# One core, two transformer blocks and a 32-expert layer in fp32: the router's chain, the first gather, the residual and one weight unit rearranged

## What is computed

```python
h = h + mixed @ w_out                       # (256,1024) @ (1024,1024)
xt = rms_norm(h, norm2_gain)
group_logits = xt @ w_route_group + b_g     # 4 groups
exp_logits = xt @ w_route_expert + b_e      # 32 experts, 8 a group
g_idx = argmax(group_logits)                # one group a token
top_v, top_i = top_k(exp_logits[g_idx], 2)  # two experts in it
w = softmax(top_v) * softmax(group_logits)[g_idx]
for e in experts:                           # D_EXPERT = 512
    y[tokens of e] += w * ((silu(xt @ w_gate[e]) * (xt @ w_up[e])) @ w_down[e])
return rms_norm(h + y, final_gain)
```

## Time and profile before

| | |
|---|---|
| median of 3 runs | 1062.4 us (1061.07 to 1064.08) |
| the profiled execution's own time | 1058.74 us |
| its span | 1056.7 us |
| busy: PE, DVE, ACT, POOL | 86%, 42%, 30%, 2% of the span |
| HBM read | 290.77 MB, mean 279 GB/s with what is written |
| chain that ended last, by engine | PE 54%, DMA 35%, DVE 6%, ACT 2% |

### The profile page before, as it was taken

The page is one execution under the profiler, slowest core; times in us unless marked ns, Lnnn a source line. Parts: engine busy times, 40 slices in busy tenths (PEclk is TensorE's granted clock), DMA queues, the critical chain, the costliest instruction groups (busy, mean ns, idle before and its releaser), DMA issues.

```text
span 1056.7 us, 18049 instructions
## 1 busy us (share of the span) xinstructions
PE 908.8 (86%) x7830; PEld 647.1 (61%) x7830; DVE 441.0 (42%) x555; ACT 317.3 (30%) x400; POOL 19.0 (2%) x36
## 2 busy tenths in 40 slices
PE   5999999999999999999989997676868577677875
PEld 5999988999998878999978732121313122121311
DVE  4677778666565448995757400000101000010102
ACT  4466664643443337544522300000000000000001
POOL 1300000000000000000000100000000000000000
PEclk9999999999999999999998998999889989898888
DMA  9993424456545354442057899999999999999994
GB/s 338 269 351 110 160 81 160 159 182 204 173 163 220 136 199 160 160 161 80 5 201 263 356 370 421 421 421 422 421 422 421 422 421 421 421 422 421 423 421 183
DMA packets 83398, 294.97 MB, mean 279 GB/s; under 512 B 5887, under 2 KB 33167, under 8 KB 58624
## 3 DMA queue, kind: packets, MB, share of 16 engines
q1 hardware_dynamic: 78240, 284.18, 68.9%
q10 hardware_dynamic: 3552, 6.08, 1.6%
q0 software_dynamic: 1536, 3.68, 1.3%
HBM read 290.77 MB, written 4.10 MB: 279 GB/s over the span
## 4 chain that ended last, share of the span: by engine, by line
PE 54%; DMA 35%; DVE 6%; ACT 2%; SPq 2%; issue 1%; DVEq 0%; ACTq 0%
DMA arena<-in_w_down 16%; PE psum L960 13%; PE psum L962 13%; PE psum L961 13%; DMA arena<-in_w_gate 10%; DMA arena<-in_w_up 8%; PE psum L1485 3%; PE psum L1280 3%; SPq L813 2%; PE psum L1505 2%; PE psum L935 1%; DVE ring_rounded L1942 1%; PE psum L927 1%; PE psum L1035 1%; PE psum L1474 1%
## 5 line engine op out<-in xcount | busy, mean ns | idle before, releaser
L1485 PE MATMUL psum<-arena,featL 128*32 128x512 f32 x1024 | 181.6, 692 | 63.4 <-DMA arena<-in_w_up 47.1
L1942 DVE TENSOR_TENSOR ring_rounded<-arena,hi_rounded 128x2048 fp32r<-128x2048 f32 x77 | 176.0, 2290 | 91.2 <-ACT hi_rounded L1590 90.1
L1590 ACT ACTIVATE hi_rounded<-arena 128x2048 fp32r<-128x2048 f32 x77 | 146.6, 1912 | 156.6 <-PE psum L962 52.1
L960 PE MATMUL psum<-hi_rounded,featT_rounded 128*128 128x256 f32 (+1 forms) x560 | 165.5, 296 | 5.9 <-DVE featL_rounded L1958 3.9
L961 PE MATMUL psum<-ring_rounded,featT_rounded 128*128 128x256 f32 (+1 forms) x560 | 163.2, 291 | 0.0
L962 PE MATMUL psum<-hi_rounded,featL_rounded 128*128 128x256 f32 (+1 forms) x560 | 163.1, 291 | 0.0
L1485 PEld LDWEIGHTS psum<-arena,featL 128*32 128x32 f32 x1024 | 40.8, 122 | 197.5 <-DMA arena<-in_w_up 87.1
L1505 PE MATMUL psum<-arena,featT 128*32 128x512 f32 x496 | 89.1, 653 | 41.1 <-DMA arena<-in_w_down 36.3
L960 PEld LDWEIGHTS psum<-hi_rounded,featT_rounded 128*128 128x128 f32 x560 | 108.6, 194 | 9.3 <-DVE ring_rounded L1942 4.2
L961 PEld LDWEIGHTS psum<-ring_rounded,featT_rounded 128*128 128x128 f32 x560 | 108.8, 194 | 1.2
L962 PEld LDWEIGHTS psum<-hi_rounded,featL_rounded 128*128 128x128 f32 x560 | 108.6, 194 | 1.3
(11 more groups left out here) (282 smaller groups left out, 1138.4 us busy)
## 6 DMA issues: line engine op xcount, KB each, us to landing
arena<-in_w_gate SPq DMA_DIRECT2D x75, 1024.0 KB, 26.2
arena<-in_w_up SPq DMA_DIRECT2D x75, 1024.0 KB, 26.6
arena<-in_w_down SPq DMA_DIRECT2D x63, 1024.0 KB, 26.9
arena<-in_w_in SPq DMA_DIRECT2D x14, 2048.0 KB, 9.1
arena<-in_w_down SPq DMA_DIRECT2D x5, 2048.0 KB, 7.6
arena<-in_w_out SPq DMA_DIRECT2D x4, 2048.0 KB, 8.3
arena<-in_w_in SPq DMA_DIRECT2D x4, 1024.0 KB, 9.7
t_copies<-arena ACTq DMA_DIRECT2D x1, 2048.0 KB, 8.2
```

The lines of the kernel that those rows point to most:

```text
L960: mm(o, lhs[0], rhs[0], start=start, stop=False, skip_group_check=True)
L1485: ins = mm(psum[32 * j:32 * j + 32, MB[4 + m], :], xg[:, 4 * half + k, 32 * j:32 * j + 32], quad[place(q)][j][:, 512 * k:512 * k + 512], s ...
L1590: fn(high, view, ACT.Copy).then_inc(hi_ready, 1)
L1942: tt(low, view, high.bitcast(F32), ALU.subtract).then_inc(lo_ready, 1)
```

## The change

Five things are changed.

1. The second unit of `wo2` is stored as two blocks of 256 columns, each by a DMA of its own. A block is then free as soon as its own chunk is done, so quad 3's piece 0 is issued behind `wo2` (1, 0). Quad 3's piece 3, which goes where the rounded chunk (0, 1) was, is issued behind `wo2` (0, 1).
2. PE starts `ybank` with identity times `x`, in place of the products of zeros; the zeroing on POOL and the four fillers ahead of them are gone. The final add on DVE is gone, and ACT and DVE read `ybank` in PSUM.
3. Since `x` is then free, quad 5's piece 0 goes there, and no longer waits for `pieces_read` but for those products (`scattered`) and for `xn`.
4. The router: ACT squares 768 columns ahead and 256 at the end; PE adds the logits of the first 256 columns ahead of the last transposes; both tiles' ranks are in one bank, come before the count, and DVE turns them into `rank` and `G` before it touches the count; fillers go from six to three.
5. The gather has three steps (slices 0-1, 2-3, 4-7); the third stands behind the first 16 gate products.

At the end ACT squares halves of 512 columns from PSUM and adds their sums through the bias of the root.

```diff
+    add("dve", "rank")
     add("dve", "count")
-    for t in range(NT):
-        add("dve", "rank", t)
...
+        quad.append([x[:].rearrange("p t d -> p (t d)")])
...
-        for n in range(2):
-            unit(("wo2", n), (0, DK, 512, kxn(A["w_out_2"], 512 * n, 512)))
+        unit(("wo2", 0), (0, DK, 512, kxn(A["w_out_2"], 0, 512)))
+        unit(("wo2", 1), (0, DK, 256, kxn(A["w_out_2"], 512, 256)), (2048, DK, 256, kxn(A["w_out_2"], 768, 256)))
...
+        ONCE = (2, 1, 1, 1)
+
+        def once(r, pair, q, j):
+            return isinstance(r, int) and isinstance(pair, int) and pair * 12 + q < NQ + ONCE[j]
+
+        def quad_place(r, pair, q, j):
 
             if not isinstance(r, int):
                 return PLACES[q % NQ]
-            if isinstance(pair, int) and pair * 12 + q <= NQ:
-                return (*PLACES, NQ)[q]
-            return PLACES[(q - 1) % NQ]
...
+            if once(r, pair, q, j):
+                return (*PLACES, NQ, NQ + 1)[q]
+            return PLACES[(q - ONCE[j]) % NQ]
...
+        GATHERS = ((6, (0, 1)), (5, (2, 3)), (7, (4, 5, 6, 7)))
+        GATHERED_AT = ((0, 0), (0, 2), (1, 0))
...
                     wait_filled(sp, "wo2", 0, 1)
                     load_quad(0, 0, 2, pieces=range(3))
+                    load_quad(0, 0, 3, pieces=(3,))
                     wait_filled(sp, "wo2", 1, 0)
                     load_quad(0, 0, 2, pieces=(3,))
+                    load_quad(0, 0, 3, pieces=(0,))
                     wait_filled(sp, "wo2", 1, 1)
-                    load_quad(0, 0, 3)
+                    load_quad(0, 0, 3, pieces=(1, 2))
                     wait_filled(sp, "logit", NT - 1)
                     load_quad(0, 0, NQ, pieces=(3,))
-                    for q in range(NQ + 1, 12):
-                        load_quad(0, 0, q, 4 * (q - NQ - (q <= 2 * NQ)))
+                    sp.wait_ge(xn_ready, 2 * NT)
+                    sp.wait_ge(scattered, 2 * NT)
+                    load_quad(0, 0, NQ + 1, pieces=(0,))
+                    load_quad(0, 0, NQ + 1, pieces=(1, 2, 3))
+                    for q in range(NQ + 2, 12):
+                        load_quad(0, 0, q, 4 * (q - NQ))
...
+            add_logits(0)
+            wait_emptied(pe, "wo2", 1, 1)
+            for k in range(2):
+                for t in range(NT):
+                    ins = tr(last_T[:, NT * k + t, :], x[:, t, (6 + k) * P:(7 + k) * P], ident)
+            end(ins)
+            for j in range(1, 4):
+                add_logits(j)
...
-            busy(4)
-            pe.wait_ge(gt_ready, 1)
             for t in range(NT):
                 for n in range(2):
-                    ins = mm(ybank[t, n], GT[:, t, :], dd[:, n, :], start=True, stop=False, skip_group_check=True)
+                    ins = mm(ybank[t, n], ident, x[:, t, 512 * n:512 * n + 512], start=True, stop=False, skip_group_check=True)
                     ins.then_inc(scattered, 1)
 
+            b = begin("rank")
+            pe.wait_ge(route_ready, 1)
+            mm_halves(b[:, 0:E], con("before"), selr[:, 0, :], True, True)
+            mm_halves(b[:, E:2 * E], con("ones"), selr[:, 0, :], True, False)
+            end(mm_halves(b[:, E:2 * E], con("before"), selr[:, 1, :], False, True))
...
-            busy(6)
-            wait_emptied(pe, "rank", NT - 1)
+
+
+            busy(3)
+            wait_emptied(pe, "rank")
...
+                pe.wait_ge(onehot_ready, n + 1)
+                gather(0)
+                gather(1)
                 for m in range(2):
                     for half in range(2):
-                        pe.wait_ge(xg_ready, 2 * n + half + 1)
+                        if m == 0 and half == 1:
+                            if isinstance(n, int) and n == 0:
+                                wait_emptied(pe, "count")
+                            gather(2)
                         q = 6 * gp + 2 * m + half
                         for k in range(4):
+                            if m == 0 and (half, k) in GATHERED_AT:
+                                pe.wait_ge(xg_ready, 3 * n + GATHERED_AT.index((half, k)) + 1)
...
+            wait_emptied(act, "wo2", 1, 0)
+            for t in range(NT):
+                part = st[:, 14 + t:15 + t]
+                a.link(fn(xn[:, t, 0:768], x[:, t, 0:768], ACT.Square, accum_out=part))
+                a.link(fn(part, part, ACT.Identity, scale=1.0 / D, bias=eps_col[:, 0:1]))
+            wait_emptied(act, "wo2", 1, 1)
+            for t in range(NT):
+                s = st[:, 6 + t:7 + t]
+                a.link(fn(xn[:, t, 768:], x[:, t, 768:], ACT.Square, accum_out=s))
+                fn(s, s, ACT.Sqrt, scale=1.0 / D, bias=st[:, 14 + t:15 + t]).then_inc(rms_ready, 1)
...
-            for n in range(2):
-                for t in range(NT):
-                    dve.wait_ge(scattered, 4 * NG + (2 * n + t + 1))
-                    xs = x[:, t, 512 * n:512 * n + 512]
-                    tt(xs, xs, psum[:, MB[2 * t + n], :], ALU.add).then_inc(resid_done[t], 1)
```

More of the change, by code:

```diff
@@ L334, in build @@
     who_of = dict(fills)
-    last = {index[key] % 8 for key in (("rank", 0), ("rank", 1), ("count",))}
+    last = [index[key] % 8 for key in (("rank",), ("count",))]
     MB = [b for b in range(8) if b not in last]
-    MB += sorted(last)
+    MB += last
     with ExitStack() as ctx:
@@ L673, in build @@
             chunk(("p2", n // 2), n % 2, cols256(("p2", n // 2), n % 2), ring[(n + len(RW_ORDER)) % 3], ("p2", n // 2, n % 2))
-        for n in range(4):
-            chunk(("wo2", n // 2), n % 2, cols256(("wo2", n // 2), n % 2), W_RING[n % 3], ("wo2", n // 2, n % 2))
+        for c in range(2):
+            chunk(("wo2", 0), c, cols256(("wo2", 0), c), W_RING[c], ("wo2", 0, c))
+        for c in range(2):
+            chunk(("wo2", 1), c, lambda of, c=c: wview(("wo2", 1), c, of), W_RING[(2 + c) % 3], ("wo2", 1, c))
         before, taken = [], {}
@@ L1416, in _, with add_logits @@
                     resid_T(3, j - 1, ("wo2", (j - 1) // 2, (j - 1) % 2))
-            resid_T(3, 3, ("wo2", 1, 1))
+            last_T = begin("nt", 3, 3).rearrange("p (k q) -> p k q", q=P)
             logits = [begin("logit", t) for t in range(NT)]
-            for j in range(4):
+            def add_logits(j):
                 wait_emptied(pe, "nt", 3, j)
@@ L1485, in moe_group @@
                                 ins = mm(psum[32 * j:32 * j + 32, MB[4 + m], :], xg[:, 4 * half + k, 32 * j:32 * j + 32],
-                                         quad[place(q)][j][:, 512 * k:512 * k + 512], start=half == 0 and k == 0,
+                                         quad[place(q, j)][j][:, 512 * k:512 * k + 512], start=half == 0 and k == 0,
                                          stop=half == 1 and k == 3, skip_group_check=True)
@@ L1505, in down @@
                     return mm(psum[32 * j:32 * j + 32, MB[4 + half], :], hhT[:, k, 32 * j:32 * j + 32],
-                              quad[place(q)][j][:, at_:at_ + 512], start=k == 0, stop=k == 3, skip_group_check=True)
+                              quad[place(q, j)][j][:, at_:at_ + 512], start=k == 0, stop=k == 3, skip_group_check=True)
                 q = 6 * gp + 4
@@ L1879, in _ @@
                         moe_round(r)
-            squares(4, lambda t: act.wait_ge(resid_done[t], 2))
+                        act.wait_ge(scattered, r * (4 * NG) + (4 + 4 * NG))
+                        fn(st[:, 12:13], eps_col[:, 0:1], ACT.Copy)
+            fn(warm[:], eps_col[:, 0:1], ACT.Sqrt)
+            for n in range(2):
+                for t in range(NT):
+                    act.wait_ge(scattered, 4 * NG + (2 * n + t + 1))
+                    s, half = st[:, 8 + t:9 + t], st[:, 10 + t:11 + t]
+                    a.link(fn(xn[:, t, 512 * n:512 * n + 512], psum[:, MB[2 * t + n], :], ACT.Square,
+                              accum_out=s if n else half))
+                    if n == 0:
+                        fn(half, half, ACT.Identity, scale=1.0 / D, bias=eps_col[:, 0:1]).then_inc(squared, 1)
+                    else:
+                        act.wait_ge(squared, t + 1)
+                        fn(s, s, ACT.Sqrt, scale=1.0 / D, bias=half).then_inc(rms_ready, 1)
         @block.vector
@@ L2405, in _, with one_hot @@
             red(e2, m2g, AX, ALU.add).then_inc(e2_ready, 1)
+            wait_filled(dve, "rank")
+            dve.wait_ge(route_ready, 1)
+            empty(stt(rank, bank("rank")[:, 0:NT * E].rearrange("p (t e) -> p t e", t=NT), CHOSEN, selr, ALU.add, ALU.mult), "rank")
+            def one_hot(es):
+                slots = con("slot").unsqueeze(1).unsqueeze(1).to_broadcast([P, NT, EG, CAP])
+                tt(G, slots, rank[:, :, es].unsqueeze(3).to_broadcast([P, NT, EG, CAP]), ALU.is_equal).then_inc(onehot_ready, 1)
+            one_hot(slice(0, EG))
             wait_filled(dve, "count")
             empty(red(rt[:, 606:607], bank("count")[:, 0:E], AX, ALU.max), "count")
+            nc.vector.tensor_copy(cnt[:, 0:1], rt[:, 606:607]).then_inc(count_ready, 1)
```

(12 more changed lines are left out.)

69 lines of the change are left out of this document (33 added, 36 removed).

## The result

The changed kernel took 1053.78 us (median of 4 runs, 1053.47 to 1054.92) beside 1062.52 us for the kernel before (4 runs, 1061.07 to 1064.08): the medians are 8.7 us apart, and the recorded ratio is 0.9925, 95% interval 0.9903 to 0.9946, which is 8.0 us less. In a later series on one chip it was 1053.85 us (6 runs) beside 1061.73 us (21 runs), 7.9 us less, ratio 0.9923 (0.9900 to 0.9946). The forecast was 6.7 us less, at 1055.7 us, with a range from 1052.8 to 1058.9.

What follows compares the result with a forecast made beforehand. The experts' part was taken to be bound by the stream of weights. Stream -6.5, stragglers +0.6 and norm -0.8 gave -6.7 us, so 1062.4 - 6.7 = 1055.7 us, with a range from 1052.8 to 1058.9.

Steps and rivals of the forecast that it cites:

- the two holes: Stretches 589 to 593 and 606 to 612, where the weight stream stands still; together 7.04 us, the most it can give.
- Hole A: 589 to 593, ended when quad 3 can go out; 2.25 us lost, closed by issuing pieces earlier.
- The router and the gather: Ahead of the experts' products: gather begins 2.4 us earlier, its first two steps take 1.9 us, gate products begin at 601.4.
- the place's load: Quad 5's piece 0 into `x`: goes out near 598 and lengthens the queue by 2.49 us, dry at 606.2.
- The restart's cost: From SP's issue to full flow, 1.54 us: flow back at 606.7, hole 0.5 us; 1.0 by the skill page.
- Stragglers: Late DMA engines no longer catch up in hole B, which is carried to the end: costs 0.6 us, bounds 0 and 1.3.
- hole B: 606 to 612, until quad 5's first piece can go out; 4.79 us lost, forecast to shrink to 0.5.
- The norm: Last norm: DVE's adds go, ACT has four rounds of 0.93 us in place of two; gain 0.8 us.
- The clock didn't fall in the router: Rival: with seven fillers gone, PE's clock falls to 0.50 from 599.5 on, giving 1059.9 us; chance 0.08.
- The unshortened chain: Rival: the router gets no shorter as one wait replaces another, only the gather's split helps, 1058.1 us; chance 0.08.
- PE became the bound: Rival, slower: PE bounds the experts' group loop; at a mean clock of 0.60, 1120 us; chance 0.03.

Runs made afterwards that it cites:

- e1: Kernel before with only the second `wo2` unit as two blocks and quad 3's pieces 3 and 0 issued early: 1059.11 us, ratio 0.9982 to the kernel before.
- e2: Changed kernel with all four pieces of quad 3 issued behind `wo2` (1, 1), as before: 1054.19 us, ratio 0.9930 to the kernel before.
- e4: Changed kernel without the place in `x`, so quad 5's piece 0 waits for PE's reading: 1055.36 us, ratio 0.9944 to the kernel before.
- e12: Changed kernel with quad 3 issued late and no place in `x`: 1057.52 us, ratio 0.9957 to the kernel before.
- e7: The kernel before, unchanged, profiled and timed again: 1061.74 us, ratio 1.0002 to the kernel before.
- e5: Changed kernel with the last norm as before (DVE copies `ybank` into `x`, ACT squares 1024 columns): 1053.32 us, ratio 0.9927 to the kernel before.
- e6: Changed kernel with 15 fillers in place of three ahead of the gather: 1056.56 us, ratio 0.9952 to the kernel before.
- e9: Changed kernel with one filler and no small ACT steps between the last norm's squares: 1053.50 us, ratio 0.9917 to the kernel before.
- e11: Changed kernel with the edits of e9 and e10 together: 1055.77 us, ratio 0.9927 to the kernel before.
- e3: Changed kernel with the third gather step ahead of the first gate products: 1053.67 us, ratio 0.9920 to the kernel before.
- e8: The changed kernel, unaltered, profiled and timed again: 1053.85 us, ratio 0.9923 to the kernel before.
- e10: Changed kernel with the second tile's two stores issued by ACT in place of SP: 1053.36 us, ratio 0.9922 to the kernel before.

## Why the prediction was right, point by point

**What bounds.** Right. The stretch 640 to 1000 is unchanged, and all that was won lies where the stream stood still: the two holes held 7.05 us and hold 0.7.

**Hole A.** Forecast closed, measured 426 GB/s. e1 adds what the text had only in the sum: closing it alone is worth nothing while the restart is late (9.22 us lost with and without it), and 1.8 us beside the other parts (e2). In the same way the place in `x` is worth 2.4 us of lost time beside them (e4) and 0.8 once quad 3 is late (e12 against e2).

**The router and the gather.** Counted from t0, the forecast was: gather 21.5, first gate product 23.4, the place's load near 20, restart 27.2. Measured: 21.49, 23.38, 19.98, 27.07. The parts were off against each other by up to 0.2: three fillers took 0.94 for 0.8, which the other steps made up for.

**The restart's cost.** 0.5 us of hole forecast, 0.7 measured (0.6 in the stretch shown). The Trainium skill, "DMA: Bandwidth & Descriptors", section "Anatomy of one DMA", has about 2.0 us for a DMA issued from GpSimd, and puts most of it behind the last byte. The loads here are issued by SP, and a hole ends with the first bytes, so the prediction's estimate of 1.0 us from it is for another path and another wait; the trace's 0.7 lies between, nearer to the row's 0.5.

**Stragglers.** The first of the two terms of the sum that failed; the norm's is the other. I forecast that closing hole B costs 0.6 us, because late DMA engines can't catch up in it. The last 5.06 us before the last landing, in the kernel before again, in the changed one, and in the changed one again:

```profile
1038.00:1043.06 5.06, 2.09 (x4) 0.27 (x4) 0.00 (x0) 0.00 (x0) 0.00 (x0) 1.00 0.59 246
```

```profile
1031.80:1036.86 5.06, 2.09 (x4) 0.28 (x4) 0.00 (x0) 0.00 (x0) 0.00 (x0) 1.00 0.60 251
```

```profile
1034.37:1039.43 5.06, 2.09 (x4) 0.28 (x4) 0.00 (x0) 0.00 (x0) 0.00 (x0) 1.00 0.61 256
```

They lose 2.1, 2.0 and 2.0 us, and the earlier trace rows has 2.9 with 183 GB/s. So the changed kernel loses no more at the end than the one before; the first profile of before happened to lose 0.8 more. In twelve of the fourteen profiles the last 5.06 us lose 1.9 to 2.3 us, with the late hole wide open (e1 1.9, e7 2.1) and nearly closed (changed kernel 2.0 and 2.0). In two they lose 2.9 us: in the first profile of before and in e12, where the hole is nearly closed. What decides it is open; the hole doesn't. With it, M fell by 7.2 us (mean of two profiles each, 463.7 to 456.5) where 5.9 were forecast: 2.4 and 4.1 in the holes, 0.5 at the end, 0.2 in small gaps. The 0.5 is mostly the first profile's chance loss again. The time lost fell from 9.2 to 2.6, by 6.6 us, where 6.5 were forecast for the stream: so it is the term of the stragglers that was off, by 1.1 us.

**The norm.** Forecast 0.8 us at the reciprocal and at the end. It was 1.1 at the reciprocal (ACT's rounds took 0.90 and began at once) and about nothing at the end in the pairs compared here: 14.7 and 15.0 before, 14.7 and 15.4 after. The step that failed is to count the reciprocal's gain as the end's. "DVE's last steps keep their length", and they did (3.13 and 3.12 us from the reciprocal), but the sum has no term for the stores behind them. From DVE's last step to the end of the span it is 2.8, 3.1, 3.4 (e5) and 4.3 us (e1) with the old norm, and 3.6 to 4.6 with the new one. So the stores alone vary by as much as the norm's gain. Leaving out e2, e4, e6 and e9 for their clock, the end is at 15.3 on average with the old norm (four profiles) and at 14.9 with the new (six, e11's among them); what the norm is worth there, between nothing and its 1.1 us, is not resolved. It is not shown what holds the stores.

**The sum.** From t0 to the end of the span the profiles have 478.7 and 478.3 us before, and 471.3 and 471.8 after: 7.0 less, beside 6.7 forecast. The two misses (M fell by 1.3 us more than forecast, and the end behind it came 0.2 later in place of 0.8 sooner, so 1.0 the other way) nearly cancelled. That the profiles' sum came so close is luck in part. The medians say 8.7 and 7.9 less, with intervals of about 2.4 us to either side; the rest of 0.9 us or more isn't explained by anything in the profiles, and needn't exist.

**The rivals.** The clock didn't fall in the router. The unshortened chain didn't come; e3 shows what half of it would have cost. PE became the bound nowhere: in 640 to 1000 it is busy 265.53 us, 1.9 more than before.

**Why t0 moved.** The level of a profile depends on the part ahead of t0, where the change leaves the arithmetic alone. The rows from 530 to t0 in the first profile of before, in the changed kernel, in e8 and in e10:

```profile
530.00:577.98 47.98, 41.47 (x801) 38.19 (x797) 29.80 (x49) 14.26 (x26) 0.00 (x0) 0.89 0.63 243
```

```profile
530.00:580.26 50.26, 43.74 (x815) 40.69 (x812) 30.74 (x50) 14.69 (x26) 0.00 (x0) 0.83 0.60 232
```

```profile
530.00:583.01 53.01, 45.97 (x884) 42.78 (x880) 33.16 (x54) 15.37 (x27) 0.00 (x0) 0.84 0.57 220
```

```profile
530.00:577.89 47.89, 40.18 (x811) 36.99 (x806) 30.32 (x50) 14.53 (x26) 0.00 (x0) 0.93 0.63 243
```

At a mean granted clock of 0.93 and 0.89 the stretch takes 48 us, at 0.83 and 0.84 it takes 50 and 53. In the serial scan of the second block PE works in short pieces (in these rows 40 to 46 us busy of 48 to 53), and its clock stands at 0.50 for 3 to 17 us, more in one execution than in the next: 10 and 14 us in the two profiles of before, 17 in both of the changed kernel. The clock isn't all of it. From SP's first `cst` load of the experts (540.90, 540.55, 543.43 and 540.50 in the four) to t0 it is 37.1, 39.7, 39.6 and 37.4 us; e8's other 2.9 us lie ahead of that load, and what they are isn't shown. I had taken the difference from the profile and the level from the median, and that kept this out of the forecast.

## What to carry to other kernels

Where a stream of loads is the bound, cost a change by two times: when the queue runs dry, and when it can restart. A hole closed ahead of an unchanged restart is worth nothing (e1), and parts that fill the same hole can't be added: taking quad 3's early issue away costs 1.8 us, the place in `x` 2.4, both together 2.5 (e2, e4, e12). Read such differences from milestones in the profile that both kernels share, and sum traffic over short stretches, not over one long one with a rounded rate. Here the time lost up to t0 + 34 repeated within 0.1 us and the last landing within 0.8, where six to twelve timed runs resolved two.

## What the hardware showed that I had not expected

The landing of a long stream's last load varied by 0.8 us between two profiles of the same kernel, since some DMA engines finish late: the last 5.06 us carry 176 to 264 GB/s in the fourteen profiles in place of 421, at a DMA share of 0.44 to 0.61 in the four profiles of the two kernels. Of four stores of 256 KB at the end, the longest issue took between 0.37 us (e11) and 1.88 us (e3) where 0.33 is usual, as the second, third or fourth of them, and moving two to another queue left the end within its spread (14.8 and 14.3). And TensorE's granted clock fell to 0.50 near the last landing in four of the fourteen profiles, after the same waits as in the others, which put the last norm 0.4 to 1.5 us later.
